# Two transformer blocks on one core: where tile 1's transposes stand, and how LayerNorm and the norms are issued

## The chip, the cores and the metric

The kernel runs on one core of a Trainium2 chip. Its five instruction streams are TensorE (PE: matmuls and transposes; PEld is its weight load), ScalarE (ACT), VectorE (DVE), GpSimd (POOL) and the DMA queue that SyncE (SP) issues. Each stream runs its instructions strictly in the order in which they were written; streams meet only in semaphores. The metric is the device time of one execution in microseconds (us), lower is better. Before: 1430.33 us, median of 3 runs (1429.98 to 1430.45).

## The reference, cut to what matters

The input x is 256 tokens by 1024 features in fp32. It goes through a first block of two layers and then through a second block of two layers.

```python
# first block, for each of 2 layers
h = x @ w_in;  a_out, b_out = attention(h), gating(h)
x = layer_norm(ALPHA * x + concat(a_out, b_out) @ w_o)              # "ln 1"
gate, up = split(x @ w_ffn_in);  ffn = (silu(gate) * up) @ w_ffn_out
ple = (p @ w_ple) * sigmoid(x @ w_ple_gate)                         # the gated embedding
x = layer_norm(ALPHA * x + ffn + ple)                               # "ln 2"
# second block, for each of 2 layers
h = modulate(rms_norm(x), sh1, sc1)                                 # xn * (1 + scale) + shift
x = x + g1 * mixer(h)                                               # even layer, then odd layer
h = modulate(rms_norm(x), sh2, sc2)
x = x + g2 * squared_relu_mlp(h)
```

layer_norm is (x - mean) * rsqrt(var + 1e-5) * g + b over the 1024 features of a token; rms_norm is x * rsqrt(mean(x*x) + 1e-6) * w.

## The kernel before

**Tiles.** The 256 tokens are two tiles of 128 tokens, called tile 0 and tile 1 (t in the code). X holds them with tokens on the partitions. A linear layer needs its input with features on the partitions, so PE transposes the tile in eight 128x128 blocks (line 1466). ACT copies the result from PSUM into XTH, rounded to PE's fp32r format (the "high half"), and DVE subtracts it from the original into XTL (the "low half"). Weights are split alike: they land in RAW, ACT writes the high half (`high`) and DVE the low half (`low`, line 1764, in WB). A product is three matmuls: high x high (line 1441), high x low (1442), low x high (1443).

**Items.** Weights come in chunks of up to 512 columns and each chunk in items of 4 feature blocks, so a chunk over 1024 features is two items, and an item on one tile is 12 matmuls. `advance()` issues loads, high halves and low halves ahead; `lows()` issues the pending low halves. While `cur["lag"]` is set, low halves wait until a matmul needs them or `lows()` is called.

**linear2.** `linear2` runs two chunks (items ia[0], ia[1], then ib[0], ib[1]) and starts with tile 0 alone: its tile-0 part is ia[0], ia[1], ib[0], after which comes tile 1. Its argument `mid` issues tile 1's transposes and, in the second block, its modulation. `mid_at` says behind which item of the first chunk; it is 0, so they stand behind ia[0]. With `pad`, dummy bf16 matmuls (line 1426) run ahead of transposes or matmuls.

**LayerNorm.** `ln_tile` issues on DVE two bn_stats (line 2027) and bn_aggr (line 2030), on POOL the root as two small steps (lines 1363 and 1365: scale and add, then power -0.5), and on DVE `ln_apply`: (x - mean) * g (line 2037) and then * rsqrt + b (line 2040). Both wait for the root.

**The rms norm.** `norm_tile` issues a square with sum on ACT, the root on POOL (the same two lines), and `norm_apply` on DVE (line 2045, writes MIX). `norm_mod`'s `go(t)` then issues the transposes of MIX on PE and the modulation: four feature blocks on ACT, four on DVE (line 1863), high halves on ACT, low halves on DVE (line 1869, XTL).

**What sets the order.** The program is a list `order` filled by the calls in the code; every engine takes its own part of it in that order. Nothing is scheduled later. `linear` with touter=True does a whole chunk for tile 0 and then for tile 1; its evacuation function `put` runs after each tile. `gated_put` is such an evacuation in the second block (lines 2124 and 2128 on DVE), `last` that of an FFN or MLP.

## Time and profile before

| what | us |
|---|---|
| median of 3 runs | 1430.33 |
| the profiled execution | 1430.49 |
| its span, first to last instruction | 1428.7 |
| PE busy | 1342.2 (94%) |
| DVE busy | 941.8 (66%) |
| ACT busy | 657.2 (46%) |
| POOL busy | 109.8 (8%) |

The profiled execution is 0.16 us above the median; 1.8 us of it lie outside the span. PE is busy in 94% of the span, and its mean granted clock is 0.984 of full speed: in a few stretches it falls to half. The weights are 268 MB read at 188 GB/s over the span. Dummy matmuls count as busy.

In the timelines below a row is: start (us from the start of the span), duration, engine, line, operation, out<-in, shapes, count, and in brackets the engine's idle time before it with what ended that. Rows of one kind that follow each other are merged with their count.

### The profile page before, as it was taken

The page shows a single profiled execution, that of the slowest core. Times are in us where ns is not written, and L with a number is a line of the kernel's source. Part 1 is how long each engine was busy: PE and PEld are TensorE (multiplying, and loading weights), DVE is VectorE, ACT ScalarE, POOL GpSimd, SP SyncE. Part 2 cuts the span into 40 slices and gives each one's busy share as a digit, 9 for nine tenths or more (in the row PEclk, how much of TensorE's full clock was granted, in tenths as well). Part 3 has the DMA queues.
Part 4 walks back from the last instruction along what each step waited for, and adds up shares of the span by engine and source line. Part 5 has one row for each costly group of instructions (what it writes and reads, how often), then busy time and mean ns, then how long its engine had stood idle before and what let it go on. Part 6 is the DMA issues. An engine that isn't in the chain of part 4 may idle for free.

```text
span 1428.7 us, 16545 instructions
## 1 busy us (share of the span) xinstructions
PE 1342.2 (94%) x6684; PEld 1105.1 (77%) x6684; DVE 941.8 (66%) x1249; ACT 657.2 (46%) x886; POOL 109.8 (8%) x156
## 2 busy tenths in 40 slices
PE   6999999999989999999798898999998988999998
PEld 6767888887867788888598776888886866788886
DVE  4857677766675777775757857776766776554444
ACT  4544533333463543333365454454544554454542
POOL 1010000000020000000114300000002320000000
PEclk9999999999999999999998999999999998999999
DMA  9505577773712667776153213767673530355550
GB/s 363 199 1 206 209 308 293 295 279 126 272 60 77 227 245 294 292 295 220 61 183 104 90 56 120 293 240 290 238 292 114 181 118 1 118 206 188 188 184 30
DMA packets 40236, 269.87 MB, mean 189 GB/s; under 512 B 4544, under 2 KB 4560, under 8 KB 11872
## 3 DMA queue, kind: packets, MB, share of 16 engines
q1 hardware_dynamic: 37712, 259.31, 48.8%
q0 software_dynamic: 2304, 8.46, 1.6%
q8 instruction: 53, 0.87, 0.2%
q10 hardware_dynamic: 144, 1.05, 0.2%
q14 instruction: 23, 0.19, 0.0%
HBM read 267.75 MB, written 1.05 MB: 188 GB/s over the span
## 4 chain that ended last, share of the span: by engine, by line
PE 81%; DVE 11%; ACT 3%; issue 2%; POOL 1%; DMA 1%; SPq 0%; POOLq 0%; ACTq 0%; DVEq 0%
PE ps L1441 23%; PE ps L1443 23%; PE ps L1442 23%; PE ps L1466 4%; PE ps L1551 2%; DVE WB L1764 2%; PE ps L1527 1%; PE ps L1454 1%; PE ps L1426 1%; ACT WB L1564 1%; DMA RAW<-W 1%; DVE st L2027 1%; DVE X L2037 1%; DVE st L1957 1%; DVE X L2040 1%
## 5 line engine op out<-in xcount | busy, mean ns | idle before, releaser
L1764 DVE TENSOR_TENSOR WB<-RAW,WB 128x2048 fp32r<-128x2048 f32 (+4 forms) x210 | 453.2, 2161 | 267.4 <-ACT WB L1564 267.3
L1564 ACT ACTIVATE WB<-RAW 128x2048 fp32r<-128x2048 f32 (+4 forms) x210 | 379.7, 1810 | 232.8 <-PE ps L1443 219.6
L1441 PE MATMUL ps<-WB,XTH 128*128 128x512 f32 (+3 forms) x1176 | 457.9, 389 | 20.0 <-DVE XTL L1769 13.0
L1443 PE MATMUL ps<-WB,XTL 128*128 128x512 f32 (+3 forms) x1176 | 448.2, 381 | 0.0
L1442 PE MATMUL ps<-WB,XTH 128*128 128x512 f32 (+3 forms) x1176 | 447.5, 381 | 0.0
L1441 PEld LDWEIGHTS ps<-WB,XTH 128*128 128x128 f32 x1176 | 223.8, 190 | 60.6 <-DVE XTL L1769 13.3
L1443 PEld LDWEIGHTS ps<-WB,XTL 128*128 128x128 f32 x1176 | 222.9, 190 | 38.4
L1442 PEld LDWEIGHTS ps<-WB,XTH 128*128 128x128 f32 x1176 | 223.8, 190 | 34.9
L1441 PE MATMUL ps<-WB,HTH 128*128 128x512 f32 (+1 forms) x452 | 178.4, 395 | 2.5 <-DVE HTL L1845 2.0
L1443 PE MATMUL ps<-WB,HTL 128*128 128x512 f32 (+1 forms) x452 | 177.7, 393 | 0.0
L1442 PE MATMUL ps<-WB,HTH 128*128 128x512 f32 (+1 forms) x452 | 177.6, 393 | 0.0
L1823 DVE SCALAR_TENSOR_TENSOR ACC<-RAW,colv,ACC 128x512 f32<-128x512 f32 x168 | 126.1, 751 | 5.1
L1564 ACT ACTIVATE HTH<-ps 128x512 fp32r<-128x512 f32 (+1 forms) x58 | 32.1, 585 | 159.6 <-PE ps L1466 159.4
L1441 PEld LDWEIGHTS ps<-WB,HTH 128*128 128x128 f32 x452 | 85.1, 188 | 22.2 <-DVE HTL L1845 2.4
L1443 PEld LDWEIGHTS ps<-WB,HTL 128*128 128x128 f32 x452 | 85.1, 188 | 19.6
L1442 PEld LDWEIGHTS ps<-WB,HTH 128*128 128x128 f32 x452 | 85.3, 189 | 19.1
L1363 POOL TENSOR_SCALAR st<-st 128x1 f32<-128x1 f32 (+3 forms) x42 | 22.9, 544 | 1002.0 <-DVE st L2030 538.6
L1564 ACT ACTIVATE GB<-ps 128x512 f32<-128x512 f32 (+1 forms) x94 | 46.4, 499 | 92.6 <-PE ps L1443 92.6
L1564 ACT ACTIVATE E<-ps,st 128x128 f32<-128x128 f32 (+1 forms) x104 | 42.4, 420 | 75.3 <-DVE st L1967 75.3
L1426 PE MATMUL ps<-cstb 128*128 128x512 bf16 x228 | 63.9, 398 | 0.0
L1845 DVE TENSOR_TENSOR HTL<-ps,HTH 128x512 fp32r<-128x512 f32 x54 | 35.8, 687 | 39.9 <-ACT HTH L1564 39.9
L1365 POOL TENSOR_TENSOR st<-st,cst 128x1 f32<-128x1 f32 (+3 forms) x42 | 48.3, 1150 | 3.5
(177 smaller groups left out, 1043.4 us busy)
## 6 DMA issues: line engine op xcount, KB each, us to landing
RAW<-W SPq DMA_DIRECT2D x220, 1024.0 KB, 4.9
RAW<-W SPq DMA_DIRECT2D x14, 768.0 KB, 4.3
RAW<-W SPq DMA_DIRECT2D x12, 728.0 KB, 6.0
VEC<-vecd POOLq DMA_DIRECT2D x10, 512.0 KB, 7.2
RAW<-W SPq DMA_DIRECT2D x8, 512.0 KB, 3.5
RAW<-W SPq DMA_DIRECT2D x4, 576.0 KB, 3.6
GB<-xTd ACTq DMA_DIRECT2D x1, 1024.0 KB, 7.8
X<-xd SPq DMA_DIRECT2D x1, 1024.0 KB, 16.1
```

The source lines that it names most:

```text
L1363: eng.tensor_scalar(x, x, scale, eps, ALU.mult, ALU.add).then_inc(*own.up())
L1365: eng.tensor_tensor(x, x, MH.to_broadcast([128, x.shape[1]]), ALU.pow).then_inc(*up("rsqrt", key))
L1426: eng.matmul(banks[b][:, :], identb, cstb[:, 0:512], start=True, stop=True)
L1441: eng.matmul(ps, xh, hi[:, j, c0:c0 + cw], start=first and j == 0, stop=False)
L1442: eng.matmul(ps, xh, lo[:, j, c0:c0 + cw], start=False, stop=False)
L1443: op = eng.matmul(ps, xl, hi[:, j, c0:c0 + cw], start=False, stop=last and j == n - 1)
L1466: op = eng.transpose(banks[b][0:rows, j * 128:j * 128 + 128], src, ident)
L1551: op = eng.matmul(banks[b][:, c0:c0 + dv], PET[:, u["i"], blk * 128:blk * 128 + 128], val, start=(j == 0), stop=(j == len(lst) - 1))
L1564: return eng.activation(dst, src, f, **k)
L1764: eng.tensor_tensor(WB[:, it["raw"], 0:w], RAW[:, it["raw"], 0:w], WB[:, it["high"], 0:w].bitcast(F32), ALU.subtract).then_inc(*up("wl", n))
L1823: op = eng.scalar_tensor_tensor(out=ACC[:, a, :], in0=view[:, j, :], scalar=cond[:, kt:kt + 1], in1=ACC[:, a, :], op0=ALU.mult, op1=ALU.add)
L1845: eng.tensor_tensor(HTL[:, r2:r2 + 2, :], banks[b][:, :].rearrange("p (n q) -> p n q", n=2), HTH[:, r2:r2 + 2, :].bitcast(F32), ALU.subtra ...
```

## The change

There are six edits:

1. `ln_apply` becomes `ln_scale`, which waits for the statistics but not for the root, and `ln_shift`, which waits for the root.
2. `linear2` gets mid_at=1 in the gated embedding (`w_ple_gate`, both layers) and in the second block's four uses: tile 1's transposes stand behind ia[1] instead of ia[0]. The first block's own `w_in` keeps 0.
3. In the first block, tile 1's ln 1 is issued between the two chunks of `w_ple`, with one `advance` (a weight item) between `ln_scale` and `ln_shift`.
4. At the end of the first block tile 0's rms norm is issued ahead of tile 1's LayerNorm root on POOL and ahead of `ln_scale` on DVE; modulation of tile 0 stands between `ln_scale` and `ln_shift`.
5. In the mixers' output projection, tile 1's `gated_put` comes ahead of tile 0's modulation `go(0)`, and low halves are issued late (`lag`), behind the norms. 
6. Between the second block's layers, `go(0)` stands between the two halves of tile 1's `gated_put`.

```diff
-        def ln_tile(key, t, after, between=None):
+        def ln_tile(key, t, after, between=None, before=None, halfway=None):
             sts, mv = col(12), col(2)
             do("ln_stats", key, t, sts, mv, after)
+            if before:
+                before()
             do("rsqrt", ("ln", key), mv[:, 1:2], 1.0, 1e-5, ("ln_mv", key))
             if between:
                 between()
-            do("ln_apply", key, t, mv)
+            do("ln_scale", key, t, mv)
+            if halfway:
+                halfway()
+            do("ln_shift", key, t, mv)
             return [("ln", key)]
...
-        def norm_tile(t, after):
+        def norm_sums(t, after):
             g = uid()
             ss = col(1)
             do("norm_sq", g, t, ss, after)
             do("rsqrt", ("nt", g), ss, 1.0 / D, 1e-6, ("norm_sq", g))
-            do("norm_apply", g, t, ss)
-            hn[t] = ("hn", g)
+
+            def apply():
+                do("norm_apply", g, t, ss)
+                hn[t] = ("hn", g)
+            return apply
...
-            x_n[1] = ln_tile((i, 1, 1), 1, rw[1])
+            for c in range(2):
+                ...
+                run(linear("w_ple", "p", [[("pl", i)], [("pl", i)]], put))
+                if c == 0:
+                    x_n[1] = ln_tile((i, 1, 1), 1, rw[1], halfway=lambda: advance(1))
...
-            run(linear2("w_ple_gate", "x", xt_w, [put_g(0), put_g(1)], mid1, pad=(0, 3)))
+            run(linear2("w_ple_gate", "x", xt_w, [put_g(0), put_g(1)], mid1, pad=(0, 3), mid_at=1))
...
-                    elif t:
-                        norm_tile(0, x_n[0])
-                        go(0, pad=14)
-                x_n[t] = ln_tile((i, 2, t), t, [("add_out", (i, t, c)) for c in range(2)], between)
+                before = norm_sums(0, x_n[0]) if t and i else None
+                x_n[t] = ln_tile((i, 2, t), t, [("add_out", (i, t, c)) for c in range(2)], between, before,
+                                 (lambda: go(0, pad=14)) if t and i else None)
...
             def put(t, b, done):
+                gput(t, b, done)
                 if t:
                     go(0)
-                gput(t, b, done)
-                if t:
                     advance(1)
                     norm_tile(1, xg[1])
+
+            cur["lag"] = True
             run(linear(nm_out, "x", xo_w, put, touter=True, mid=lambda: norm_tile(0, xg[0])))
+            cur["lag"] = False
+            lows()
...
-                    gen = linear2("mlp_w1_2", "x", xt_w, [put_f(0), put_f(1)], mid, pad=(11, 0))
+                    gen = linear2("mlp_w1_2", "x", xt_w, [put_f(0), put_f(1)], mid, pad=(11, 0), mid_at=1)
...
             def last(t, done):
-                if t and i == 0:
-                    go(0)
                 for c in range(2):
                     gated_put(i, c, 1, xg)(t, acc4[t][c][0], done[c])
+                    if t and c == 0 and i == 0:
+                        go(0)
...
-            def ln_apply(key, t, mv):
+            def ln_scale(key, t, mv):
                 xs, n = X[:, t, :], 3 * (key[1] - 1)
-                on.wait_ge(*at("rsqrt", ("ln", key)))
+                on.wait_ge(*at("ln_mv", key))
                 on.wait_ge(*at("vec0", (key[0], n)))
-                on.wait_ge(*at("vec1", (key[0], n + 1)))
                 eng.scalar_tensor_tensor(out=xs, in0=xs, scalar=mv[:, 0:1], in1=VEC[:, 0:1024], op0=ALU.subtract,
-                                         op1=ALU.mult).then_inc(*own.up())
-                on.wait_ge(*own.at())
+                                         op1=ALU.mult).then_inc(*up("ln_scaled", key))
+
+            def ln_shift(key, t, mv):
+                xs, n = X[:, t, :], 3 * (key[1] - 1)
+                on.wait_ge(*at("rsqrt", ("ln", key)))
+                on.wait_ge(*at("vec1", (key[0], n + 1)))
+                on.wait_ge(*at("ln_scaled", key))
                 eng.scalar_tensor_tensor(out=xs, in0=xs, scalar=mv[:, 1:2], in1=VEC[:, 1024:2048], op0=ALU.mult,
                                          op1=ALU.add).then_inc(*up("ln", key))
```

The same mid_at=1 is added in the second block's two `w_in` projections. The rows of ACT and of SP stand in the same order as before; on POOL one root changes its place (edit 4).

PE, the first projection of the second block (`even_w_in_2`; ia is 384 columns wide, ib 288), from the last matmul of ia[0] on tile 0. Before:

```order
L1443 MATMUL ps<-WB,XTL 128x384
L1426 MATMUL ps<-cstb 128x512 x2
L1466 MATMUL ps<-cst,MIX 128x128 x8
L1441 MATMUL ps<-WB,XTH 128x384
L1442 MATMUL ps<-WB,XTH 128x384
```

The same stretch now, from the last matmul of ia[1] on tile 0:

```order
L1443 MATMUL ps<-WB,XTL 128x384
L1426 MATMUL ps<-cstb 128x512 x2
L1466 MATMUL ps<-cst,MIX 128x128 x8
L1441 MATMUL ps<-WB,XTH 128x288
L1442 MATMUL ps<-WB,XTH 128x288
```

The two dummies and the eight transposes moved behind 12 more matmuls of tile 0; between them and tile 1's first matmul there are 12 matmuls (ib[0]) instead of 24.

DVE at the end of the first block, from tile 1's additions of the FFN (L2068 before, L2088 now) on. Before:

```order
L2068 TENSOR_TENSOR X<-X,ps 128x512 x2
L2027 BN_STATS st<-X 128x6 x2
L2030 BN_AGGR st<-st 128x2
L2045 TENSOR_SCALAR MIX<-X,st 128x1024
L1863 TENSOR_SCALAR GB<-ps,modc 128x128 x4
L1869 TENSOR_TENSOR XTL<-GB,XTH 128x4x128 x2
L2037 SCALAR_TENSOR_TENSOR X<-X,st,VEC 128x1024
L2040 SCALAR_TENSOR_TENSOR X<-X,st,VEC 128x1024
L1764 TENSOR_TENSOR WB<-RAW,WB 128x1536
```

Now:

```order
L2088 TENSOR_TENSOR X<-X,ps 128x512 x2
L2043 BN_STATS st<-X 128x6 x2
L2046 BN_AGGR st<-st 128x2
L2065 TENSOR_SCALAR MIX<-X,st 128x1024
L2052 SCALAR_TENSOR_TENSOR X<-X,st,VEC 128x1024
L1879 TENSOR_SCALAR GB<-ps,modc 128x128 x4
L1885 TENSOR_TENSOR XTL<-GB,XTH 128x4x128 x2
L2060 SCALAR_TENSOR_TENSOR X<-X,st,VEC 128x1024
L1780 TENSOR_TENSOR WB<-RAW,WB 128x1536
```

Tile 1's first LayerNorm step (L2052) moved in front of tile 0's modulation (L1879); the second stayed.

DVE in the even layer's output projection, from tile 0's norm_apply (L2045 before, L2065 now) to tile 1's. Before:

```order
L2045 TENSOR_SCALAR MIX<-X,st 128x1024
L1764 TENSOR_TENSOR WB<-RAW,WB 128x2048
L1863 TENSOR_SCALAR H<-ps,modc 128x128 x4
L1869 TENSOR_TENSOR XTL<-H,XTH 128x4x128 x2
L2124 TENSOR_TENSOR MIX<-ps,VEC 128x512
L2128 TENSOR_TENSOR X<-X,MIX 128x512
L1764 TENSOR_TENSOR WB<-RAW,WB 128x2048
L2045 TENSOR_SCALAR MIX<-X,st 128x1024
L1820 TENSOR_SCALAR ACC<-RAW,colv 128x512
```

Now:

```order
L2065 TENSOR_SCALAR MIX<-X,st 128x1024
L2144 TENSOR_TENSOR MIX<-ps,VEC 128x512
L2148 TENSOR_TENSOR X<-X,MIX 128x512
L1879 TENSOR_SCALAR H<-ps,modc 128x128 x4
L1885 TENSOR_TENSOR XTL<-H,XTH 128x4x128 x2
L1780 TENSOR_TENSOR WB<-RAW,WB 128x2048
L2065 TENSOR_SCALAR MIX<-X,st 128x1024
L1780 TENSOR_TENSOR WB<-RAW,WB 128x2048
L1836 TENSOR_SCALAR ACC<-RAW,colv 128x512
```

Tile 1's gated_put went ahead of tile 0's modulation, one low half (L1780) behind that modulation and the other behind tile 1's norm_apply.

## Rows read from the trace of the kernel before

**Rows 1.** The page's busy time by engine.
```profile
PE 1342.2 (94%) x6684; PEld 1105.1 (77%) x6684; DVE 941.8 (66%) x1249; ACT 657.2 (46%) x886; POOL 109.8 (8%) x156
```

**Rows 2.** PE's waits: waiter, releaser, us in total, times, longest.
```profile
PE ps L1466 <- DVE MIX L2045: 15.5, 6, 3.5
PE ps L1466 <- DVE X L2040: 4.0, 6, 0.9
```

**Rows 3.** Timelines, first layer, tile 0's ln 1: DVE, POOL, PE.
```profile
118.90 0.21 DVE L2030 BATCH_NORM_AGGREGATE st<-st 128x2 f32<-128x12 f32 x1
...
120.13 1.28 DVE L2037 SCALAR_TENSOR_TENSOR X<-X,st,VEC 128x1024 f32<-128x1024 f32 x1 [1.02 <-POOL st L1365]
...
119.27 0.19 POOL L1363 TENSOR_SCALAR st<-st 128x1 f32<-128x1 f32 x1 [41.26 <-DVE st L2030]
119.55 0.55 POOL L1365 TENSOR_TENSOR st<-st,cst 128x1 f32<-128x1 f32 x1
...
122.79 1.09 PE L1466 MATMUL ps<-cst,X 128*128 128x128 f32 x8 [0.60 <-DVE X L2040]
```

**Rows 4.** Timelines, second block's latent norms: DVE, POOL.
```profile
729.03 0.62 DVE L2088 SCALAR_TENSOR_TENSOR MIX<-MIX,st,small 128x384 f32<-128x384 f32 x1 [0.72 <-POOL st L1365]
...
729.08 0.62 POOL L1363 TENSOR_SCALAR st<-st 128x1 f32<-128x1 f32 x1
```

**Rows 5.** Timeline of PE, first layer, the gated embedding.
```profile
131.92 1.04 PE L1426 MATMUL ps<-cstb 128*128 128x512 bf16 x4
133.75 1.09 PE L1466 MATMUL ps<-cst,X 128*128 128x128 f32 x8 [0.79 <-DVE X L2040]
135.94 0.50 PE L1441 MATMUL ps<-WB,XTH 128*128 128x512 f32 x1 [1.11 <-DVE WB L1764]
...
142.00 0.58 PE L1441 MATMUL ps<-WB,XTH 128*128 128x512 f32 x1
```

**Rows 6.** Timelines, first block's end and second block's start: DVE, PE.
```profile
697.81 0.75 DVE L2045 TENSOR_SCALAR MIX<-X,st 128x1024 f32<-128x1024 f32 x1 [1.85 <-POOL st L1365]
...
705.24 1.75 DVE L1764 TENSOR_TENSOR WB<-RAW,WB 128x1536 fp32r<-128x1536 f32 x1
...
698.62 1.10 PE L1466 MATMUL ps<-cst,MIX 128*128 128x128 f32 x8 [2.96 <-DVE MIX L2045]
...
702.26 0.45 PE L1441 MATMUL ps<-WB,XTH 128*128 128x384 f32 x1 [0.39 <-DVE XTL L1869]
...
708.56 1.97 PE L1466 MATMUL ps<-cst,MIX 128*128 128x128 f32 x8 [3.50 <-DVE MIX L2045]
...
715.74 0.34 PE L1441 MATMUL ps<-WB,XTH 128*128 128x384 f32 x1
```

**Rows 7.** Stretch: us, busy PE, PEld, DVE, ACT, POOL, PE's clock, DMA.
```profile
707.00:714.00 7.00, 5.44 (x20) 5.44 (x21) 4.92 (x8) 3.32 (x7) 4.38 (x10) 0.52 0.00 0
```

**Rows 8.** Timelines, even layer, entry of its MLP: DVE, POOL, PE.
```profile
885.24 2.28 DVE L1764 TENSOR_TENSOR WB<-RAW,WB 128x2048 fp32r<-128x2048 f32 x1
...
889.43 2.33 DVE L1823 SCALAR_TENSOR_TENSOR ACC<-RAW,colv,ACC 128x512 f32<-128x512 f32 x3
...
886.59 0.98 POOL L1363 TENSOR_SCALAR st<-st 128x1 f32<-128x1 f32 x1 [8.53 <-ACT MIX L1564]
...
883.26 0.50 PE L1441 MATMUL ps<-WB,XTH 128*128 128x512 f32 x1 [0.89 <-DVE XTL L1869]
...
886.12 0.60 PE L1426 MATMUL ps<-cstb 128*128 128x512 bf16 x2
889.06 1.09 PE L1466 MATMUL ps<-cst,MIX 128*128 128x128 f32 x8 [2.33 <-DVE MIX L2045]
...
895.48 0.39 PE L1441 MATMUL ps<-WB,XTH 128*128 128x512 f32 x1
```

**Rows 9.** Timeline of PE: entries of the odd layer's mixer and MLP.
```profile
1091.46 1.09 PE L1466 MATMUL ps<-cst,MIX 128*128 128x128 f32 x8 [3.52 <-DVE MIX L2045]
...
1240.84 1.09 PE L1466 MATMUL ps<-cst,MIX 128*128 128x128 f32 x8 [2.33 <-DVE MIX L2045]
```

More of the change, by code:

```diff
@@ L701, in norm_tile @@
             do("rsqrt", ("nt", g), ss, 1.0 / D, 1e-6, ("norm_sq", g))
-            do("norm_apply", g, t, ss)
-            hn[t] = ("hn", g)
+            def apply():
+                do("norm_apply", g, t, ss)
+                hn[t] = ("hn", g)
+            return apply
+        def norm_tile(t, after):
+            norm_sums(t, after)()
         def norm_mod(layer, k, after):
@@ L853, in program, with put @@
                        mid=lambda: x_n.__setitem__(0, ln_tile((i, 1, 0), 0, rw[0]))))
-            x_n[1] = ln_tile((i, 1, 1), 1, rw[1])
+            for c in range(2):
+                def put(t, b, done, c=c):
+                    do("ple", (i, c, t), t, c, b, [done, sgo])
+                    give(b, ("ple", (i, c, t)))
+                run(linear("w_ple", "p", [[("pl", i)], [("pl", i)]], put))
+                if c == 0:
+                    x_n[1] = ln_tile((i, 1, 1), 1, rw[1], halfway=lambda: advance(1))
             x_w = x_n
@@ L859, in program @@
             xt_w = xt_n
-            for c in range(2):
-                def put(t, b, done, c=c):
-                    do("ple", (i, c, t), t, c, b, [done, sgo])
-                    give(b, ("ple", (i, c, t)))
-                run(linear("w_ple", "p", [[("pl", i)], [("pl", i)]], put))
             def mid1():
@@ L1015, in program @@
                 run(linear2("even_w_in_2", "x", xt_w, [put_lat(0, 0, 384), put_lat(1, 384, 672)], mid,
-                            pad=(10, 0)))
+                            pad=(10, 0), mid_at=1))
                 lnw = [[], []]
@@ L1133, in program @@
                 run(weave(chain(linear2("odd_w_in_2", "x", xt_w, [put_H("odd", c, c * 512, c * 512 + 512, dw[c])
-                                                                  for c in range(2)], mid, pad=(11, 0)), part((3, 4))),
+                                                                  for c in range(2)], mid, pad=(11, 0), mid_at=1), part((3, 4))),
                           [[ch[0, 0][0]], [gs[0], ch[0, 1][0], ch[0, 0][1]], [gs[1], ch[0, 1][1], ch[1, 0][0]],
@@ L2030, in ln_stats @@
                 eng.bn_aggr(mv, sts.rearrange("p (c k) -> p c k", k=6)).then_inc(*up("ln_mv", key))
-            def ln_apply(key, t, mv):
+            def ln_scale(key, t, mv):
+                xs, n = X[:, t, :], 3 * (key[1] - 1)
+                on.wait_ge(*at("ln_mv", key))
+                on.wait_ge(*at("vec0", (key[0], n)))
+                eng.scalar_tensor_tensor(out=xs, in0=xs, scalar=mv[:, 0:1], in1=VEC[:, 0:1024], op0=ALU.subtract,
+                                         op1=ALU.mult).then_inc(*up("ln_scaled", key))
+            def ln_shift(key, t, mv):
                 xs, n = X[:, t, :], 3 * (key[1] - 1)
                 on.wait_ge(*at("rsqrt", ("ln", key)))
-                on.wait_ge(*at("vec0", (key[0], n)))
                 on.wait_ge(*at("vec1", (key[0], n + 1)))
-                eng.scalar_tensor_tensor(out=xs, in0=xs, scalar=mv[:, 0:1], in1=VEC[:, 0:1024], op0=ALU.subtract,
-                                         op1=ALU.mult).then_inc(*own.up())
-                on.wait_ge(*own.at())
+                on.wait_ge(*at("ln_scaled", key))
                 eng.scalar_tensor_tensor(out=xs, in0=xs, scalar=mv[:, 1:2], in1=VEC[:, 1024:2048], op0=ALU.mult,
@@ L2147, in vector_program @@
                          p_split=p_split, soft=soft, joint=joint, differ=differ, normalise=normalise, sgw_mask=sgw_mask,
-                         gating=gating, residual=residual, ln_stats=ln_stats, ln_apply=ln_apply,
+                         gating=gating, residual=residual, ln_stats=ln_stats, ln_scale=ln_scale, ln_shift=ln_shift,
                          norm_apply=norm_apply, gate=gate, ffn=ffn, add_out=add_out, lambdas=lambdas,
```

## The prediction

> **What bounds the kernel now.** I read the page's busy times first: PE is busy for 1342.2 of 1428.7 us [rows 1], so nothing outside PE's own path is worth much, and the most that any reordering can take out is the 86.5 us in which PE stands. Then PE's waits. Two of them touch the change: the transposes in front of the modulation wait for norm_apply (six times, 15.5 us) and those behind a LayerNorm wait for its last step (six times, 4.0 us) [rows 2]. The timelines of the places where these waits lie come next. At each the reader is to see the same picture: PE has finished tile 0's first item, has 24 more tile-0 matmuls that need nothing from tile 1, and stands in front of tile 1's transposes all the same, because its stream is in order [rows 5, 6, 8, 9].
>
> **LayerNorm's first step (edit 1).** Before, DVE stood from 119.11 to 120.13 for the root [rows 3]: 1.02 us, and with two steps of 1.28 the tile was ready 3.62 after the statistics. The step now starts at once. But POOL begins its root 0.16 after the statistics, when the step, which reads X and VEC from SBUF, already runs. What a root does under such an operation is in [rows 4]: the same POOL step that takes 0.19 alone took 0.62, from 0.05 after the start of a DVE scalar_tensor_tensor with two SBUF inputs to 0.05 after its end. So I let the root begin at the end of the first step: 1.3 + 0.75 for the root, then the second step. The tile is ready 3.35 after the statistics: 0.25 to 0.3 won, not 1.0. The ends are 0 (the root loses more than that) and 1.0 (it is not held up); I take 0.3 since [rows 4] is the same kind of DVE operation against the same POOL instruction.
>
> The Trainium skill ("SBUF — State Buffer", section "SBUF: two separate sides") says that a DVE operation with two SBUF inputs and a GpSimd operation that reads SBUF exclude each other for a whole instruction, whichever began first. This is a rule against edit 1, and the 0.62 of [rows 4] agrees with it. By it the sum is the one below; without it, that of the second rival.
>
> **Transposes behind ia[1] (edits 2 and 3), gated embedding, twice.** Tile 1's first matmul began at 142.00 [rows 5]. Now: tile 0's transposes waited 0.60 [rows 3], and 0.3 of it goes, so ia[0] ends at 131.6 in place of 131.92. Tile 1's statistics end 3.62 before 133.7, less 0.3: 129.8. First step to 131.15, then a low half (2.28, the length of the one in [rows 8]) to 133.4. That is ia[1]'s, and PE stands for it for 1.8, a new wait in place of the 0.79 and 1.11 of before [rows 5]. ia[1] takes 2.85 (12 matmuls: 883.26 to 886.12 in [rows 8]), to 136.25; four dummies 0.95; eight transposes 0.9; ib[0] 2.7; three dummies 0.5: tile 1 starts at 141.3. That is 0.7 earlier. LayerNorm's second step, with the root behind a low half too, ends at about 135.2, in time for the transposes at 137.2. The other layer has the same order and the same waits within 0.1: 0.7 again. Bounds 0 to 1.7, the whole of the removed waits less 0.2.
>
> **ln 2 of the first layer.** Only edit 1 acts, on tile 0, and what follows is a chain on DVE: 0.2.
>
> **Start of the second block (edits 1, 2, 4).** Before, norm_apply waited 1.85 for two roots in a row, the LayerNorm's and then its own [rows 6]. Its own now goes first and is ready long before; DVE is free at 697.81 - 1.85 = 695.96, or 695.75 with the 0.2 of tile 0's LayerNorm. The transposes start at 696.55 in place of 698.62 and, 3.64 later as before, tile 0's first matmul at 700.2 in place of 702.26: 2.05. The LayerNorm step in front of the modulation hides in the 1.1 in which DVE waits for the transposes. ia[0] at 384 columns takes 2.15 (three quarters of 2.86), to 702.35. ia[1]'s low half started 2.98 after tile 0's first matmul [rows 6]; one LayerNorm step of 1.28 in front of it is gone, so it starts at 701.9 and ends at 703.65: a new wait of 1.3. ia[1] to 705.8, two dummies to 706.25, transposes; tile 1's first matmul is held by the modulation, 3.64 later: 709.9. Before it was 715.74. So 5.85, of which 2.05 is tile 0 and about 2.6 is the clock: after PE had stood 3.50 before 708.56 [rows 6], it was granted 0.52, its lower level of 1.2 GHz, for 7 us [rows 7], where 5.44 us of work would have taken half. Now PE stands 1.3 and 1.1 at most here, and I take the clock to stay at 2.4 GHz. Bounds 3.2 (it falls as before) to 6.5 (no lockout).
>
> **Entry of the even MLP (edits 2, 5).** Tile 1's gated_put (two operations of 512 columns, 1.4 by the 1.28 for 1024 in [rows 3]) replaces a low half (2.3) in front of tile 0's modulation, but then ACT's high half is what is late: tile 0 starts at 882.55, 0.7 before the 883.26 of [rows 8]. ia[0] ends at 885.4, when the first low half, now behind the modulation, is just ready. ia[1] runs to 888.2. Before, tile 1's root started under the second low half and took 0.98 [rows 8]; with that low half behind norm_apply and tile 1's gated_put done 3 us earlier, norm_apply ends at 887.3. Two dummies, transposes at 888.7 without a wait, ib[0] to 892.4. But now DVE owes, in a row: the low half (2.3, to 889.6), the ada products (0.5 and the 2.33 of [rows 8], to 892.4), and its part of the modulation with half of XTL, 2.0 (an estimate: the 3.64 of [rows 6] less 1.6 for the transposes and ACT's start): tile 1 starts at 894.4, having stood 2.0 for XTL. Before, 895.48: 1.1 won. Bounds 0.7 to 3.1 (no wait for XTL).
>
> **Entries of the odd layer (edits 2, 6 and 2, 5).** No ada products here. From the transposes to tile 1's first matmul it was 0.85 + 24 matmuls, 6.42 in all (889.06 to 895.48 in [rows 8]), so 1097.9 and 1247.25 from [rows 9]. In the mixer's entry one half of tile 1's gated_put now runs while DVE would stand for tile 0's transposes: tile 1's square and ia[1]'s low half come 1.4 earlier, and the latter ends at about 1088.6. PE, done with ia[0] at 1087.3 (1091.46 less the wait of 3.52 and 0.6 of dummies), stands 1.3, then ia[1] to 1091.4, dummies and transposes 1.3, ib[0] 2.8: 1095.55. In the MLP's entry likewise: ia[0] to 1237.8, low half ready at 1237.9, ia[1] to 1240.7, dummies, transposes, ib[0] to 1245.0. Each 2.3, of removed waits of 3.52 and 2.33. Bounds 1 to 3.3 each.
>
> What costs nothing: `lag` moves low halves only behind the norms, as counted; SP's queue is as before, and PE's items come in the same order, so loads only start earlier with PE.
>
> **The sum.** 0.7 + 0.7 + 0.2 + 5.85 + 1.1 + 2.3 + 2.3 = 13.15 us. The profiled execution of 1430.49 (span 1428.7 and 1.8 around it) becomes 1417.3, and the median, 0.16 lower, 1417.2.
>
> **Rivals.**
> - The root is not held up by the first step. For it: alone it takes 0.74 and fits under 1.28. Against it: [rows 4]. Each LayerNorm of tile 0 is then ready 0.7 earlier; PE's waits leave 0.3 + 0.3 + 0.4 + 0.65 of it: 1415.6.
> - The clock falls at the second block's start all the same: PE still stands in several places within 15 us. For it: it fell there before [rows 7]. Against: the two long waits are gone, and 3.52 at 1091.46 [rows 9] did not bring it down. 2.6 less: 1419.8.
> - The waits only change their name: what PE no longer waits for norms it waits for ia[1]'s low half and for XTL, so that only tile 0's parts stay: 0.3 + 0.3 + 0.2 + 2.05 + 0.7 = 3.55, so 1426.8. For it: four of the six places have such a new wait in my own working. Against: it is shorter than the old one in each.
> - Slower: the new stands have no dummies in them (before, four or two ran ahead of the wait), and the clock falls behind them. A fall costs 2.6 here. It decides from five falls on, since 13.15 / 2.6 = 5; at all six moved places, with no gain but tile 0's, 1426.8 + 15.6 = 1442. Against: the longest new stand is 2.0.
>
> **How the numbers follow.** Forecast 0.66, then 0.08, 0.17, 0.06 and 0.03. The forecast's own range is 1414.5 to 1420: the bounds above do not all fall on one side, and the stretches in the attentions in which PE has its lower clock may grow or shrink by a us or two as all moves earlier. With the first two rivals, 1412.5 to 1422. A measurement of this kernel can tell about 0.2%, 2.9 us: all cases but the last are faster by more than that, the fourth by so little that it gives a part to no change: faster 0.94, same 0.03, slower 0.03.
>
> **What would show it.** Root: POOL's first step of a LayerNorm takes about 1.2 instead of 0.19, and the second DVE step starts 2.05 behind the statistics. Transposes: PE's wait for norm_apply falls from 15.5 to about 4, and new waits for WB (about 6 in four places) and one for XTL of 2.0 appear. Clock: 1.00 over the start of the second block. Wrong if the second block's start still has the half clock, or if waits for WB or XTL exceed 3 at a place.

## The result, and the profile after

The changed kernel takes 1416.78 us in the median of 4 runs (1415.32 to 1418.49), against 1430.15 (1429.73 to 1430.45) for the kernel before beside it: ratio 0.9907, 95% interval 0.989 to 0.9924. The forecast was 1417.2 with a range of 1412.5 to 1422. A second set of five runs gave 1416.5, ratio 0.9905 (0.989 to 0.992). The profiled execution of the changed kernel took 1416.97, with a span of 1415.2 and a mean granted clock of 0.988, where before had 1428.7 and 0.984. One execution of the kernel "after - edit 1" below took 2238.17 us at a mean granted clock of 0.556; it is left out of that kernel's median.

The page's row of busy times answers to [rows 1]:

```profile
PE 1336.6 (94%) x6653; PEld 1102.3 (78%) x6684; DVE 942.4 (67%) x1249; ACT 657.0 (46%) x886; POOL 120.3 (8%) x156
```

DVE and ACT do the same work in the same time. PE's 5.6 us less are no measure of the gain: 31 records of dummy matmuls are missing here (PEld has all 6684), and fewer stretches ran at the lower clock. POOL has the same 156 instructions, and they last 10.5 us longer: the first trace of edit 1. Then PE's waits (waiter, releaser, us in total, times, longest), beside [rows 2]. Such a wait, in which PE does nothing, is called a stand below:

```profile
PE ps L1457 <- DVE WB L1780: 6.3, 5, 1.7
...
PE ps L1457 <- DVE XTL L1885: 3.3, 6, 1.3
...
PE ps L1482 <- DVE X L2060: 1.8, 4, 1.0
...
PE ps L1482 <- DVE MIX L2065: 1.6, 2, 0.8
```

The transposes' wait for norm_apply fell from 15.5 to 1.6 us and the one for LayerNorm from 4.0 to 1.8. The low halves of weights (WB) cost 2.7 in three waits before and 6.3 in five now. XTL went from 1.7 to 3.3. So 16.1 us of waits went and 5.2 came.

**Place by place.** I counted the weight matmuls in both traces and compared the start of the same one, ahead of each place and behind it. The lead that the changed kernel gains in between is what the place is worth.

| place | forecast | measured |
|---|---|---|
| gated embedding, first and second layer | 0.7 + 0.7 | 0.68 + 0.64 |
| ln 2 of the first layer | 0.2 | 0.16 |
| start of the second block | 5.85 | 5.78 |
| entry of the even MLP | 1.1 | 1.63 |
| entry of the odd layer's mixer | 2.3 | 2.03 |
| entry of the odd layer's MLP | 2.3 | 2.18 |
| sum | 13.15 | 13.10 |
| all stretches between | none | 0.4 (+1.9, -0.3, -1.8, +0.6) |

Most of the last row is the clock's: 1.6 of the +1.9 are a fall to the lower clock at 79.2 us that only before has, and 1.6 of the -1.8 are one at 896.4 us that before has not. Together 13.5, the difference of the spans.

**The root under LayerNorm's first step** (DVE, then POOL, in the first layer's tile 0 and tile 1; compare [rows 3]):

```profile
117.03 0.21 DVE L2046 BATCH_NORM_AGGREGATE st<-st 128x2 f32<-128x12 f32 x1
117.27 1.28 DVE L2052 SCALAR_TENSOR_TENSOR X<-X,st,VEC 128x1024 f32<-128x1024 f32 x1
119.28 1.29 DVE L2060 SCALAR_TENSOR_TENSOR X<-X,st,VEC 128x1024 f32<-128x1024 f32 x1 [0.72 <-POOL st L1381]
...
128.00 1.28 DVE L2052 SCALAR_TENSOR_TENSOR X<-X,st,VEC 128x1024 f32<-128x1024 f32 x1
129.21 2.28 DVE L1780 TENSOR_TENSOR WB<-RAW,WB 128x2048 fp32r<-128x2048 f32 x1
```

```profile
117.40 1.21 POOL L1379 TENSOR_SCALAR st<-st 128x1 f32<-128x1 f32 x1 [39.68 <-DVE st L2046]
118.69 0.55 POOL L1381 TENSOR_TENSOR st<-st,cst 128x1 f32<-128x1 f32 x1
...
128.06 1.28 POOL L1379 TENSOR_SCALAR st<-st 128x1 f32<-128x1 f32 x1 [8.81 <-DVE st L2046]
129.42 2.48 POOL L1381 TENSOR_TENSOR st<-st,cst 128x1 f32<-128x1 f32 x1
```

POOL's step ends when DVE's does: 1.21 in place of the 0.19 of [rows 3]. Under a low half, its power step takes 2.48 in place of 0.55. The second DVE step starts 2.04 behind the statistics; the prediction said 2.05.

**PE at the gated embedding** (tile 1's transposes and first matmul; compare [rows 5]):

```profile
120.62 1.09 PE L1482 MATMUL ps<-cst,X 128*128 128x128 f32 x8 [0.30 <-DVE X L2060]
...
131.64 0.47 PE L1457 MATMUL ps<-WB,XTH 128*128 128x512 f32 x1 [1.72 <-DVE WB L1780]
...
135.35 1.04 PE L1482 MATMUL ps<-cst,X 128*128 128x128 f32 x8
...
139.44 0.58 PE L1457 MATMUL ps<-WB,XTH 128*128 128x512 f32 x1
```

Tile 0's stand fell from 0.60 to 0.30. The two stands of 0.79 and 1.11 are one of 1.72, for the low half that the forecast had at 1.8.

**PE at the second block's start** (tile 0's transposes, tile 0's first matmul, ia[1], tile 1's first matmul; compare [rows 6]), and two stretches there with the clock in the third column from the end (compare [rows 7]):

```profile
693.32 1.09 PE L1482 MATMUL ps<-cst,MIX 128*128 128x128 f32 x8 [0.80 <-DVE MIX L2065]
696.97 0.44 PE L1457 MATMUL ps<-WB,XTH 128*128 128x384 f32 x1 [0.39 <-DVE XTL L1885]
700.52 0.41 PE L1457 MATMUL ps<-WB,XTH 128*128 128x384 f32 x1 [1.19 <-DVE WB L1780]
706.84 0.41 PE L1457 MATMUL ps<-WB,XTH 128*128 128x384 f32 x1 [1.06 <-DVE XTL L1885]
```

```profile
697.00:707.00 10.00, 7.69 (x46) 6.91 (x48) 7.94 (x11) 6.33 (x11) 4.82 (x10) 1.00 0.00 0
...
896.40:899.80 3.40, 3.40 (x9) 2.69 (x10) 3.37 (x5) 1.11 (x1) 0.00 (x0) 0.51 0.88 335
```

In a row of such a stretch stand its length, the busy us of PE, PEld, DVE, ACT and POOL, then the clock. The stand of 2.96 is down to 0.80 and the one of 3.50 is gone; what came is 1.19 and 1.06, and the clock stays at its upper level of 2.4 GHz. The second stretch is the reverse case: behind the entry of the even MLP the clock is at its lower level for 3.4 us, which it was not before. By the matmuls' starts it costs 1.6.

**PE at the MLP's and the odd layer's entries** (tile 1's first matmul of the even MLP; PE's sum of the ada products, which DVE makes; ia[1] of the odd mixer; compare [rows 8, 9]):

```profile
884.97 0.47 PE L1457 MATMUL ps<-WB,XTH 128*128 128x512 f32 x1 [1.32 <-DVE XTL L1885]
...
895.48 1.02 PE L1470 MATMUL ps<-cst,ACC 128*128 128x1 f32 x8 [1.19 <-DVE ACC L1839]
...
1079.96 0.47 PE L1457 MATMUL ps<-WB,XTH 128*128 128x512 f32 x1 [1.19 <-DVE WB L1780]
```

At the odd MLP nothing is waited for any more but 0.18 for XTL.

### The profile page after: what moved, and what is told of

Its sections match the earlier page's. It is cut to its first block, busy times and chain, and to the rows that moved or that the text cites. A ratio compares the mean times of both kernels' runs of the same rounds, so it can differ in the third digit from the quotient of the medians.

```text
span 1415.2 us, 16524 instructions
## 1 busy us (share of the span) xinstructions
PE 1336.6 (94%) x6653; PEld 1102.3 (78%) x6684; DVE 942.4 (67%) x1249; ACT 657.0 (46%) x886; POOL 120.3 (8%) x156
## 3 DMA queue, kind: packets, MB, share of 16 engines
q10 hardware_dynamic: 144, 1.05, 0.2%
HBM read 267.75 MB, written 1.05 MB: 190 GB/s over the span
## 4 chain that ended last, share of the span: by engine, by line
PE 82%; DVE 11%; ACT 3%; issue 2%; DMA 1%; POOL 1%; SPq 0%; DVEq 0%; ACTq 0%; POOLq 0%
PE ps L1457 24%; PE ps L1459 23%; PE ps L1458 23%; PE ps L1482 4%; DVE WB L1780 2%; PE ps L1567 2%; PE ps L1543 1%; PE ps L1470 1%; PE ps L1442 1%; ACT WB L1580 1%; DMA RAW<-W 1%; DVE st L1973 1%; DVE st L2043 1%; DVE SCR L1896 0%; ACT XTH L1580 0%
## 5 line engine op out<-in xcount | busy, mean ns | idle before, releaser
L1780 DVE TENSOR_TENSOR WB<-RAW,WB 128x2048 fp32r<-128x2048 f32 (+4 forms) x210 | 453.5, 2162 | 254.2 <-ACT WB L1580 254.1
L1379 POOL TENSOR_SCALAR st<-st 128x1 f32<-128x1 f32 (+3 forms) x42 | 28.6, 682 | 981.7 <-DVE st L2046 524.4
L1442 PE MATMUL ps<-cstb 128*128 128x512 bf16 x197 | 54.3, 383 | 1.9 <-issue 0.2
L1381 POOL TENSOR_TENSOR st<-st,cst 128x1 f32<-128x1 f32 (+3 forms) x42 | 52.9, 1260 | 3.5
```

The costliest lines, as they stand in the source:

```text
L1379: eng.tensor_scalar(x, x, scale, eps, ALU.mult, ALU.add).then_inc(*own.up())
L1381: eng.tensor_tensor(x, x, MH.to_broadcast([128, x.shape[1]]), ALU.pow).then_inc(*up("rsqrt", key))
L1442: eng.matmul(banks[b][:, :], identb, cstb[:, 0:512], start=True, stop=True)
L1780: eng.tensor_tensor(WB[:, it["raw"], 0:w], RAW[:, it["raw"], 0:w], WB[:, it["high"], 0:w].bitcast(F32), ALU.subtract).then_inc(*up("wl", n))
```

## Experiments

Twelve kernels, each timed in five rounds beside the kernel before; a median is of 4 to 11 executions. Medians of before in the three sets were 1430.18, 1430.38 and 1431.26. "Before +" and "after -" say on which kernel the edit was made.

| kernel | us | ratio to before, 95% interval |
|---|---|---|
| before + edit 2 | 1431.3 | 1.0011 (1.0002 to 1.0019) |
| before + edit 1 | 1431.8 | 1.0007 (0.9998 to 1.0016) |
| before + 14 dummies | 1430.25 | 1.001 (0.9999 to 1.002) |
| after - edit 2 | 1420.41 | 0.9932 (0.9918 to 0.9945) |
| after - edit 1 | 1420.3 | 0.9928 (0.9915 to 0.9942) |
| after - edit 4 | 1421.69 | 0.9939 (0.9926 to 0.9951) |
| after - edit 5 | 1417.66 | 0.9906 (0.9892 to 0.992) |
| after - edit 6 | 1419.85 | 0.9922 (0.9909 to 0.9935) |
| after, low half first | 1417.19 | 0.9909 (0.9895 to 0.9922) |
| after, ada products later | 1415.23 | 0.9897 (0.9882 to 0.9912) |
| the same - edit 5 | 1415.86 | 0.9896 (0.9879 to 0.9912) |
| after once more | 1416.5 | 0.9905 (0.989 to 0.992) |

### Before + edit 2

```diff
-            run(linear2("w_ple_gate", "x", xt_w, [put_g(0), put_g(1)], mid1, pad=(0, 3)))
+            run(linear2("w_ple_gate", "x", xt_w, [put_g(0), put_g(1)], mid1, pad=(0, 3), mid_at=1))
...
```

(and mid_at=1 at the second block's four uses)

> The kernel before with one edit alone: tile 1's transposes behind both of tile 0's chunks (mid_at=1) at all five entries. My theory (the places add up one by one, and this edit only pays where what stands in front of tile 1 on VectorE is short): in the gated embedding the low half of the second chunk is still behind tile 1's LayerNorm, so TensorE now stands in front of tile 0's second chunk, about 1.8 us lost in each of the two; start of the second block 2.4 won, of it 2.6 from the clock, which no longer falls there; MLP entry of the even layer 1.6, of the odd layer 2.5, mixer entry of the odd layer 0.9 won. Together some 3.8 won, 1426.4 us. Rival (the moved transposes carry the whole change, and the other edits are small beside it): 10 us or more won, 1420 or less.

Measured: 1431.3, no gain at all, and by the interval even 0.1% slower. PE, ia[1] in the first gated embedding and in the odd mixer, and the clock behind each:

```profile
135.84 0.77 PE L1441 MATMUL ps<-WB,XTH 128*128 128x512 f32 x1 [3.96 <-DVE WB L1764]
...
1093.57 0.77 PE L1441 MATMUL ps<-WB,XTH 128*128 128x512 f32 x1 [2.54 <-DVE WB L1764]
```

```profile
133.90:140.80 6.90, 4.96 (x12) 3.80 (x12) 4.00 (x2) 0.00 (x0) 1.17 (x2) 0.51 0.42 154
714.20:717.60 3.40, 3.34 (x11) 3.37 (x12) 2.20 (x2) 0.48 (x1) 3.35 (x6) 0.50 0.00 0
1093.10:1096.50 3.40, 2.93 (x7) 2.38 (x8) 2.68 (x3) 1.17 (x1) 3.32 (x5) 0.50 0.00 0
```

The waits were as I had them: 3.96 in place of 0.79 and 1.11 is 2.1 lost, and the MLP entries gave 1.7 and 2.4. What failed was the clock. It fell at four of the new stands (the three of these rows, and at 482.1 in the second gated embedding), and the two gated embeddings lost 4.1 and 3.4 in place of 1.8 each, the second block's start gave 0.7 in place of 2.4, the odd mixer lost 0.5 in place of winning 0.9. The rival fell too. This is the prediction's slower rival at work. In the whole change the new stands are 1.06 to 1.72 long, and at none of them did the clock fall.

### After - edit 2

```diff
-            run(linear2("w_ple_gate", "x", xt_w, [put_g(0), put_g(1)], mid1, pad=(0, 3), mid_at=1))
+            run(linear2("w_ple_gate", "x", xt_w, [put_g(0), put_g(1)], mid1, pad=(0, 3)))
...
```

(and mid_at=1 taken out at the second block's four uses)

> The changed kernel with that one edit undone: tile 1's transposes again behind the first of tile 0's chunks at all five entries, the rest stays. My theory (edits 1, 3 and 4 leave something for this one to win at the MLP and mixer entries): gated embeddings 0.1 lost each, start of the second block 5.85 won as in the whole change, MLP entries 1.1 (even) and about 1 (odd), mixer entry of the odd layer about 1.3; together some 9.3 won, 1420.9 us, so this edit is worth about 4 us in the company of the others. Rival A: the other edits bring all of it (1417, as the whole change). Rival B: without it they bring next to nothing (1427 or more).

Measured: 1420.41, half a us from the theory, but partly by balance. By the matmuls' starts against before, the gated embeddings lose 0.04 and 0.07, the start of the second block wins 6.11, the even MLP 1.64 and the odd MLP 1.2, while the odd mixer loses 0.2 in place of winning 1.3, for the clock fell there at 1082.1. PE at the start of the second block (tile 1's transposes), and the clock there:

```profile
704.60 1.09 PE L1482 MATMUL ps<-cst,MIX 128*128 128x128 f32 x8 [2.18 <-DVE MIX L2065]
```

```profile
700.00:714.00 14.00, 11.82 (x75) 11.17 (x74) 9.05 (x12) 7.57 (x14) 4.80 (x10) 1.00 0.11 37
```

So edit 2 is worth 3.6 us in company and nothing alone, but not at every place: it wins 0.7 in each gated embedding, 2.3 at the odd mixer (the fall of the clock included) and 1.0 at the odd MLP. At the even MLP it adds nothing to the others. At the start of the second block it costs 0.3, since the transposes left behind ia[0] stand for 2.18 there, and those moved bring the stands of 1.19 and 1.06.

### Before + edit 1, and after - edit 1

```diff
-            do("ln_apply", key, t, mv)
+            do("ln_scale", key, t, mv)
+            do("ln_shift", key, t, mv)
...
```

(and the two steps themselves, as in edit 1)

> The kernel before with LayerNorm's application split in two steps alone, of which the first no longer waits for the root. My theory (GpSimd's two small steps to the root take as much longer as VectorE's first step beside them lasts, as the trace of after shows at one place): each of the tile-0 stands gives back only part of the step's 1.28, the first GpSimd step reads about 1.2 instead of 0.19, and 0.3 to 0.5 is won at each of four places, 1.6 in all, 1428.5 us. Rival (the root runs beside the first step undisturbed): GpSimd's steps stay at 0.19 and 0.55, and some 0.9 is won at each stand on LayerNorm's second step, 4 to 5 us in all, 1425.5 us.

Measured: 1431.8, where the theory had 1428.5. POOL's first step in the first layer's tile 0:

```profile
118.64 1.21 POOL L1364 TENSOR_SCALAR st<-st 128x1 f32<-128x1 f32 x1 [41.10 <-DVE st L2031]
```

The rival falls on this row: the root is held up. In the first block the places gave about 1.1 us (by the matmuls' starts 0.30, 0.23, 0.15, 0.22 and 0.23). At the end the execution was only 0.8 ahead: falls of the clock at 696.3 and 887.4 that before does not have took 0.6 and 1.6, and a shorter one near 771 gave back 1.4. The median shows no gain.

The undoing, with the root awaited by the first step again:

```diff
             def ln_scale(key, t, mv):
-                on.wait_ge(*at("ln_mv", key))
+                on.wait_ge(*at("rsqrt", ("ln", key)))
```

> The changed kernel with LayerNorm's first step waiting for the root again (edit 1 undone, the order of the rest unchanged). My theory (in company the edit is worth more than alone, since at tile 1 of the gated embedding the first low half stands behind the first step, and the root is hidden under both): 0.3 lost at each of four tile-0 stands, and 0.95 more in each gated embedding; tile 0's share there adds to it: 2.9 lost in all, 1419.7 us, and GpSimd's steps read 0.19 and 0.55 again. Rival A (what the prediction's sum gave the edit): 1.0 lost, 1417.8 us. Rival B (the edit is worth nothing, as its run alone had no gain that could be measured): 1416.8.

Measured: 1420.3, 3.5 lost. PE in the first gated embedding:

```profile
121.05 1.09 PE L1482 MATMUL ps<-cst,X 128*128 128x128 f32 x8 [0.68 <-DVE X L2060]
...
132.98 0.47 PE L1457 MATMUL ps<-WB,XTH 128*128 128x512 f32 x1 [2.64 <-DVE WB L1780]
```

0.38 more at tile 0 and 0.92 more at ia[1], as expected. Rivals A and B fall. In the second gated embedding ia[1] stands 2.65, and there the clock fell (at 476.3, 1.6 us more); at the 2.64 of the first it did not. The prediction's sum held edit 1 for 0.3 in each gated embedding; it is worth 1.3 and 1.2 there without that fall, because edit 3 put a low half behind its first step, where an unawaited root matters to PE.

### Before + 14 dummies

```diff
-            mid = (lambda go=go: go(1, pad=2))
+            mid = (lambda go=go: go(1, pad=2 if i else 16))
```

> The kernel before with 14 more dummy matmuls (16 instead of 2) ahead of tile 1's transposes at the start of the second block, and nothing else: TensorE's stand there is filled, and no wait is taken away. My theory (2.6 of the 5.85 us at this place are the clock's: the engine stands 2.96 us of 6.6, and then runs 6.83 us at a granted clock of half): no stretch at half near 707 to 714, and 2.6 us won, 1427.5 us. Rival (the fall has its cause in earlier work, or comes anyway and moves): a half-clock stretch of some length within 15 us of that place, and within 0.5 us of the time before, or up to 1 slower where the dummies push work on.

Measured: 1430.25, so by the total the rival. The trace says otherwise (the second block's start, then three later stretches):

```profile
700.00:716.00 16.00, 15.24 (x89) 13.00 (x91) 11.01 (x14) 8.24 (x14) 4.80 (x10) 1.00 0.10 35
903.00:906.40 3.40, 3.40 (x10) 2.64 (x9) 3.33 (x6) 0.20 (x1) 0.00 (x0) 0.50 1.00 414
1090.80:1094.20 3.40, 3.40 (x11) 2.72 (x10) 3.35 (x6) 2.65 (x6) 3.40 (x6) 0.51 0.00 0
1240.90:1244.40 3.50, 3.50 (x12) 2.82 (x10) 2.66 (x6) 2.59 (x6) 0.00 (x0) 0.51 0.02 5
```

With the stand filled, the clock stays up, and tile 1's first matmul comes 2.57 earlier against the matmuls ahead of it: the clock's share of this place is what the prediction gave it. Then the clock falls at four places of the unchanged rest at which it had not fallen in before (these three and 1066.9), each for 1.5 to 1.6 us. It falls at 1155.6 too, and in exchange the long fall behind that place is shorter: 0.8 won between the two. Why it falls at these places is open. Single executions of this kernel ran from 1429.5 (clock 0.984) to 1435.6 (clock 0.978).

### After once more

(no edit)

> The changed kernel once more, unaltered, for a second profiled execution. My theory (the spread of a kernel's executions comes from which of TensorE's stands bring its clock down in one of them): at equal matmuls and equal waits the stretches at half clock begin elsewhere or are of other number, and the execution's time and its mean granted clock go together; 1416.8 us in the median, 1414 to 1419 in the single executions. Rival (the order of the work fixes the stretches): the same seven stretches at the same places, within 0.1 us.

Measured: 1416.5. The same waits, other stretches:

```profile
72.60:76.10 3.50, 3.50 (x10) 1.00 (x8) 1.88 (x3) 2.62 (x3) 3.48 (x4) 0.51 0.00 0
79.50:82.90 3.40, 3.40 (x15) 2.40 (x16) 1.15 (x5) 0.88 (x4) 0.00 (x0) 0.50 0.02 5
896.40:899.80 3.40, 3.40 (x19) 2.92 (x20) 3.36 (x5) 1.86 (x1) 0.00 (x0) 1.00 0.79 282
```

The fall at 896 is not there, and the first layer's attention has two in place of one. At the matmul behind each, this execution was 1.6 ahead and 1.5 behind the other. The rival falls: the same program has its falls at other stands in another execution. The second half of the theory holds for before, whose 27 executions of the first set read 1430.9 to 1432.2 at a mean clock of 0.982 (5 of them) and 1428.2 to 1428.6 at 0.986 (3). For the changed kernel's five, at 0.987 and 0.988, the figure is too coarse to tell.

### After - edit 4

```diff
-                before = norm_sums(0, x_n[0]) if t and i else None
-                x_n[t] = ln_tile((i, 2, t), t, [("add_out", (i, t, c)) for c in range(2)], between, before,
-                                 (lambda: go(0, pad=14)) if t and i else None)
+                    elif t:
+                        norm_tile(0, x_n[0])
+                        go(0, pad=14)
+
+                x_n[t] = ln_tile((i, 2, t), t, [("add_out", (i, t, c)) for c in range(2)], between)
```

> The changed kernel with edit 4 alone undone: at the start of the second block tile 0's norm has its root behind that of tile 1's LayerNorm again, and tile 0's modulation stands ahead of both LayerNorm steps. My theory: norm_apply waits 1.85 again and tile 0 loses 2.05; ia[1]'s low half is one LayerNorm step further back, so TensorE stands some 2.5 for it, as in the run with the moved transposes alone, and the clock falls behind that: tile 1's first matmul 12.7 behind tile 0's instead of 9.9, 4.9 lost in all, 1421.7 us. Rival (the moved transposes and the halfway low half carry this place, and the clock holds): only 2.05 or little more lost, 1419 us.

Measured: 1421.69, the theory's figure. PE (tile 0's transposes, ia[1], tile 1's first matmul) and the clock:

```profile
696.41 1.97 PE L1483 MATMUL ps<-cst,MIX 128*128 128x128 f32 x8 [2.75 <-DVE MIX L2066]
...
705.51 0.41 PE L1458 MATMUL ps<-WB,XTH 128*128 128x384 f32 x1 [2.22 <-DVE WB L1781]
...
713.38 0.41 PE L1458 MATMUL ps<-WB,XTH 128*128 128x384 f32 x1 [1.07 <-DVE XTL L1886]
```

```profile
706.30:709.80 3.50, 3.25 (x11) 2.73 (x11) 1.98 (x2) 0.00 (x0) 3.50 (x8) 0.51 0.00 0
```

The place lost 5.4: 2.7 to tile 0's first matmul (I had 2.05; the clock was at half at 696.1 already) and 2.7 to tile 1's. Without edit 4 the place keeps 0.4 of its 5.78, with edit 2 alone it had 0.7, and without edit 2 it has 6.11. So the gain here is edit 4's, with edit 1 beside it, and in the whole change the moved transposes have no part in it.

### After - edit 6

```diff
+                if t and i == 0:
+                    go(0)
                 for c in range(2):
                     gated_put(i, c, 1, xg)(t, acc4[t][c][0], done[c])
-                    if t and c == 0 and i == 0:
-                        go(0)
```

> The changed kernel with edit 6 undone: at the odd layer's mixer entry tile 0's modulation again ahead of both halves of tile 1's gated residual. My theory (with the transposes moved, the half residual is what delays the second chunk's low half): TensorE stands 2.5 instead of 1.2 for that low half, and tile 1's first matmul comes 0.8 later, 1417.6 us; 1.7 more if the clock falls behind that stand as in the run with the moved transposes alone, 1419.3. Rival (edit 6 is without effect here, as the low half has room): 1416.8 us.

Measured: 1419.85. PE's ia[1], and the clock:

```profile
1079.84 0.77 PE L1457 MATMUL ps<-WB,XTH 128*128 128x512 f32 x1 [2.53 <-DVE WB L1780]
```

```profile
1079.30:1082.70 3.40, 2.87 (x7) 2.32 (x8) 2.68 (x3) 1.23 (x1) 3.32 (x5) 0.50 0.00 0
```

The stand is 2.53, and in this execution the clock fell at it: 2.5 lost at the place. Theory and its addition hold.

### After - edit 5

```diff
             def put(t, b, done):
+                if t:
+                    go(0)
                 gput(t, b, done)
                 if t:
-                    go(0)
                     advance(1)
...
-            cur["lag"] = True
...
-            cur["lag"] = False
-            lows()
```

> The changed kernel with edit 5 undone: at both MLP entries tile 0's modulation again ahead of tile 1's first gated part, and low halves ahead of the norms. My theory (the moved transposes alone make the gain at these entries; in the run with them alone it was 1.7 and 2.5 us, against 1.6 and 2.2 in the whole change): nothing is lost, 0.3 won at the most, 1416.4 us. Rival (the prediction's working, in which the low half behind the modulation lets tile 0 start 0.7 earlier and tile 1's norm come before it): 0.7 lost at each of the two entries, 1418.2 us.

Measured: 1417.66, which the run's spread does not part from either 1416.4 or 1418.2; the trace decides. PE at the even MLP, tile 0's first matmul and tile 1's:

```profile
874.31 0.50 PE L1455 MATMUL ps<-WB,XTH 128*128 128x512 f32 x1 [0.88 <-DVE XTL L1883]
...
884.84 0.47 PE L1455 MATMUL ps<-WB,XTH 128*128 128x512 f32 x1 [0.69 <-DVE XTL L1883]
```

Against the matmuls ahead of the place, tile 0 is 0.70 later without edit 5, as the prediction worked out, and tile 1 is not later at all (0.05 earlier): its stand for XTL is 0.69 in place of 1.32. At the odd MLP tile 1 comes 0.18 earlier without the edit. Edit 5 wins 0.7 and gives it back 11 us on: the theory. At the even MLP edits 2 and 5 thus do not add: without edit 5 the place wins what it wins with it, without edit 2 it wins 1.64, and with edit 2 alone it won 1.7.

### After, low half first

```diff
-                    x_n[1] = ln_tile((i, 1, 1), 1, rw[1], halfway=lambda: advance(1))
+                    advance(1)
+                    x_n[1] = ln_tile((i, 1, 1), 1, rw[1])
```

> The changed kernel, in both gated embeddings with the low half of tile 0's second chunk ahead of tile 1's LayerNorm statistics instead of halfway through the LayerNorm. My theory (VectorE is what bounds this stretch: its queue is full from tile 1's statistics to the third low half, so whichever piece goes first, the sum of the pieces stays, and the root no longer runs beside a low half, which puts an idle 0.7 into the queue): TensorE's stand of 1.72 for the low half goes, but tile 1's transposes and the low half behind them come 1.1 later than now, tile 1's first matmul 0.4 later, 0.8 lost in all, 1417.6 us. Rival (the low half is what holds TensorE, and the rest has room): the 1.72 is taken out at both places less the 0.5 by which the LayerNorm is late, 1.2 won each, 1414.4 us.

Measured: 1417.19. PE: tile 1's transposes and ib[0]; ia[1] no longer waits:

```profile
134.47 1.09 PE L1483 MATMUL ps<-cst,X 128*128 128x128 f32 x8 [0.62 <-DVE X L2061]
136.67 0.50 PE L1458 MATMUL ps<-WB,XTH 128*128 128x512 f32 x1 [1.11 <-DVE WB L1781]
```

1.72 in one stand has become 0.62 + 1.11 in two; tile 1's first matmul is 0.21 and 0.20 later. DVE's queue bounds this place, so nothing is to be had from its order. The loss is half of what I expected, and the rival falls.

### After, ada products later, with and without edit 5

```diff
                 if it["name"] == "ada_w_2":
+                    if cur["hold"]:
+                        return
...
                     norm_tile(1, xg[1])
+                    cur["hold"] = True
...
-            mid = (lambda go=go: go(1, pad=2))
+            def mid(go=go):
+                go(1, pad=2)
+                cur["hold"] = False
```

> The changed kernel with the four ada products at the entry of the even layer's MLP behind tile 1's modulation instead of ahead of it on VectorE. My theory (they alone make the new stand of 1.32 us for XTL there): the stand goes, tile 1's first matmul comes 1.3 earlier, the products still end before the next low half, and the wait of 1.19 for their sum behind it stays as it is or shrinks: 1.3 won, 1415.5 us; if the half-clock stretch at 896 goes with the stand, 1.7 more. Rival (the products are as late for the sum as the modulation was for TensorE, and the wait only moves to the sum): the stand at the sum grows from 1.19 to about 2.5 and nothing is won, 1416.8 us.

> The changed kernel with the ada products behind tile 1's modulation (as in the run that did that alone) and edit 5 undone. My theory: the 1.3 of the products stays, and edit 5's absence brings 0 to 0.3 more: 1415.0 us. Rival (the products' place only paid because edit 5 had cleared VectorE's queue ahead of them): nothing better than the changed kernel, 1416.8 us or more.

Measured: 1415.23 and 1415.86. In the first the stand of 1.32 is gone, tile 1's first matmul comes 1.45 earlier against those ahead of the place, and the sum's stand is what it was:

```profile
882.03 0.47 PE L1464 MATMUL ps<-WB,XTH 128*128 128x512 f32 x1
...
892.51 1.02 PE L1477 MATMUL ps<-cst,ACC 128*128 128x1 f32 x8 [1.19 <-DVE ACC L1846]
```

The second wins 0.9 at the place: with the products moved, edit 5 is worth 0.6 there, so my theory's "0 to 0.3 more" was wrong in sign. The fall of the clock at 896 is absent in the first and there in the second, though neither has the stand for XTL:

```profile
896.20:899.50 3.30, 3.30 (x9) 2.60 (x8) 3.23 (x6) 1.91 (x1) 0.00 (x0) 0.50 0.97 340
```

By its place the first is the best version, some 1.4 us better than the changed kernel; the intervals of the totals (0.9897 against 0.9907 and 0.9905) do not part them.

## Why the prediction was right

- **The order of the readings.** PE at 94% and stands in front of tile 1's transposes in rows: the change acts there and nowhere else. One step of this reading is too narrow: the 86.5 us in which PE stands are not the most that can be had, since the 2.6 us of the clock in the prediction's own sum come out of PE's busy time. The sum over the seven places was 13.15 and came to 13.10, and the waits moved as named: 5.8 for WB in four places, where the prediction had "about 6 in four places", and norm_apply from 15.5 to 1.6. For that one it said "about 4", though its own working leaves 1.8: 15.5 less 2.05, 3.50, 2.33, 3.52 and 2.33.
- **Edit 1, the root under the first step.** Right in mechanism and size: 1.21 for POOL's step, 2.04 to the second step. (Where the prediction names the second rival for the case that the root is not held up, it means the first of its list.) The run with edit 1 alone and its undoing bear it out. What the sum did not tell is that the edit is worth three times its 1.0 once edit 3 stands behind it: leaving it out costs 3.5 (3.1 in the profiled execution).
- **Gated embedding.** 0.7 each, measured 0.68 and 0.64, with the new stand of 1.72 for 1.8.
- **Start of the second block.** 5.85, measured 5.78; the 2.6 of it for the clock measured alone as 2.57. The prediction names edits 1, 2 and 4 for it. Taking edit 4 away costs 5.4 there, and without edit 2 it is 6.11: the new stands of 1.19 and 1.06 eat what the moved transposes save. For this place the size was right and the part of the moved transposes in it was not.
- **Even MLP.** The term was too small: forecast 1.1, measured 1.63, since tile 1 waits 1.32 for XTL and not 2.0. The products that the prediction named as the cause are it: later, and the stand is gone. Behind the place the clock fell at 896 and took 1.6. No run shows the new stand as its cause: the second execution has the stand (1.35) and not the fall, and the last kernel above has the fall and not the stand.
- **Odd entries.** 2.3 each, measured 2.03 and 2.18; the stand for the low half was 1.19 in the mixer (forecast 1.3) and none in the MLP.
- **The slower rival.** Its condition, a fall behind a new stand, came true in four places of "before + edit 2" and in none of the changed kernel. Its price of 2.6 a fall was too high for most: a fall of 3.4 us cost 1.5 to 1.6, so 13.15 us would take some eight of them and not five.
- **Luck.** That the total hit to half a us is partly balance: 1.8 lost behind the even MLP against 1.9 won in the first layer's start and attention, which the change does not touch. The second execution had the balance elsewhere. The prediction's "a us or two" for the attentions in its range was the right allowance.

## What to carry to other kernels

- Price an edit in the company in which it comes. Edits 1 and 2 alone win nothing that could be measured, and taken out of the whole they cost 3.5 and 3.6 us: one shortened DVE's queue in front of tile 1, the other gave PE work meanwhile. Then price it place by place: edit 2 costs 0.3 at the start of the second block. (No run has it out at that place alone.)
- When work is moved in front of a wait on PE, list what that work itself needs (here the low half of ia[1]) and where it stands in the producer's queue. The new stand of 1.72 was readable; alone, at 3.96, it came with a fall of the clock.
- With half-clock stretches in the profile, compare kernels matmul by matmul at the changed place. A total can hide a local gain of 2.6 us, as that of the dummies did.

## What the runs showed of the hardware

- The stretches at the lower clock change their places between executions of one program, at equal waits. Most last 3.4 us and cost 1.5 to 1.6 us each while PE has work.
- New stands in front of weight matmuls, over all these kernels: at the eight of 2.22 to 3.96 us the clock fell seven times; at the many of 1.05 to 1.74 us it never fell. Length alone does not decide: of two stands in one execution, the one of 2.64 had no fall and the one of 2.65 had one, and the 3.52 of [rows 9] had none.
- A small POOL step under a DVE operation with two SBUF inputs does not end before that operation: 0.19 became 1.21 and 1.28, and the power step's 0.55 became 2.48, ending 0.4 behind the low half of 2.28 under which it had begun. A norm_apply, whose one tensor input is X, held it up too: 0.58 for the step at 692.74. One with one of its two inputs in PSUM (the XTL of line 1857 at 351.25) did not: 0.19. Between two DVE operations that follow each other at once, a waiting step still ends with the first: the one at 128.06 ended at 129.34, though the low half had begun at 129.21.
